# Keeping attention's mixed values on chip and moving their division into the probability flips

## The chip, the cores and the metric

The kernel runs on one core of one Trainium2 chip. The metric is device microseconds of one whole execution, and smaller is better. Its engines are named as in the profile: PE is the matmul engine (PEld its weight loads), DVE the vector engine, ACT the scalar engine, POOL the GpSimd engine, SP the engine whose queue issues most transfers.

## The reference, cut to what matters

One encoder layer with the same weights is applied to a prompt group (512 tokens) and a sample group (1024 tokens), both of width 1024.

```python
oa = _window_attention(qa, ka, va, sink_a)          # 8 heads of 64, 128-token windows, softmax with a sink
ob = _neighbourhood_attention(qb, kb, vb, rpb_b)    # 8 heads of 64, 2-D neighbourhoods, softmax with a bias
merged = concatenate([_rmsnorm(oa, g_out_a), _rmsnorm(ob, g_out_b)], axis=-1)
x = x + merged @ w_out
h = _rmsnorm(x, g_ffn)
x = x + expert_choice_ffn(h, w_router, w_gate, w_up, w_down)   # 16 experts, top-k by token
y = _rmsnorm(x, g_final)
```

## The kernel before

The program runs four stages one after the other, each closed by a barrier of all engines: `project` (the first linear layer), `attend` (both attentions), `mix` (norms, the w_out projection, the router), `experts` (the expert layers and the final norm). Matmuls that must be close to fp32 are made of three passes with operands split in a high and a low part (`three_pass`): high by high, high by low, low by high. A split is one ACT copy (the high part) and one DVE subtraction (the low part).

In `attend` the work is a list of 24 blocks (12 windows and 12 neighbourhoods, taken in turns), each with four head pairs: 96 units. Each engine walks the same list of steps, each lagging by some steps. In its step u, PE makes the two score matmuls of unit u (L922, into one of three score banks), turns the probabilities of unit u-2 (L932, "flips", 12 or 8 transposes into two flip banks), turns the mixed values of unit u-4 (L943), and multiplies values by flipped probabilities for unit u-3 (L963, into one bank). DVE adds mask or bias and takes the row maximum (L863, twice), inverts the sums (L870), copies half of the flips out of PSUM (L875) and scales the output by the inverted sums (L890). ACT copies the other half of the flips (L814), copies the mixed values out so that PE can turn them (L820), and takes the exponentials with their sums (L828). The scaled rows go to DRAM (`o_scratch`), 24 stores. PE fills its gaps at the end of the stage with idle matmuls (L905). In these last steps tile 0 of the stored rows is loaded and turned, and the first two of eight pieces of w_out are split.

In `mix` the rows of 12 token tiles come back from `o_scratch`. Step s works on three tiles: it projects tile s (48 matmuls of 512 columns: eight pieces j of w_out by two column halves by three passes), routes tile t = s-1, and prepares tile s+1. For the preparation ACT squares the row halves, takes the roots, multiplies the rows by the inverse roots (L1190, `ld_merged`), PE turns them (`turn_merged`, L164), ACT makes the high part (L1165) and DVE the low part (L1236, `lower`). For the routing DVE adds the projection to x (L1269), PE turns the sum (L164 with `k_p`), ACT copies it (L1144), PE multiplies by the router (L1404, L1411), DVE reduces (L1312), ACT takes exponentials, DVE scales, and PE turns the result (L1419) in front of the last piece of the step's projection. DVE and ACT take their instructions strictly in the order written. From step 9 on DVE also searches for the best tokens of the sample group between these operations. Tiles 0 and 1 are the exception: their two column groups of `merged` are projected into separate banks, and DVE multiplies by the inverse roots while adding (L1251, L1259).

## Time and profile before

| what | value |
|---|---|
| runs of the kernel | 2483.61, 2486.14, 2487.29 us (median 2486.14) |
| the profiled execution | 2484.71 us, its span 2482.9 us |
| PE busy over the span | 2434.5 us, 98% |
| DVE, ACT, POOL busy | 67%, 59%, 7% |
| `attend`, first score matmul to the last | 315.6 to 494.0 us |
| `mix`, first matmul to the start of `experts` | 502.4 to 682.6 us |

The span is from the first to the last instruction; the 1.8 us between span and time lie around it. Starts of instructions are counted from the span's start. A PE that is busy is not at its peak, since matmuls overlap; so the spacing of starts is what is read below.

### The profile page before, as it was taken

The numbers are of one execution on the slowest core, as the hardware profiler recorded it, in microseconds if no ns is written. First come the engines' busy times: TensorE is split into PE (matmuls) and PEld (weight loads), VectorE is DVE, ScalarE is ACT, GpSimd is POOL, SyncE is SP. The second block draws the span as 40 slices with busy tenths as digits, with TensorE's granted clock in tenths as the row PEclk, the third lists the DMA queues.
The fourth block names the chain that finished last, engine by engine and source line by source line (L and its number), as shares of the span: only waits on it lengthen the run. The fifth ranks groups of instructions, "written<-read, shape, count | busy, mean of one in ns | idle before, by whom it ended". The sixth has DMA issues, their size and how long they took to land.

```text
span 2482.9 us, 43086 instructions
## 1 busy us (share of the span) xinstructions
PE 2434.5 (98%) x16395; PEld 2178.7 (88%) x16395; DVE 1673.5 (67%) x2432; ACT 1456.5 (59%) x2050; POOL 163.7 (7%) x172
## 2 busy tenths in 40 slices
PE   9999999999889999999999999999999999999997
PEld 7888877777579989899998989999998989999896
DVE  6355278854776767676666767666676767666677
ACT  4332189977555656556565656555565655656574
POOL 0000000000010101101010100101010110101010
PEclk9999999999989999999999999999999999999998
DMA  7353255354376767767676767767676776767696
GB/s 250 123 177 113 62 163 202 122 186 154 111 286 224 260 224 258 240 241 247 234 248 233 250 234 248 256 230 251 223 259 226 256 244 238 251 230 253 228 325 222
DMA packets 104549, 545.29 MB, mean 220 GB/s; under 512 B 11344, under 2 KB 19920, under 8 KB 54800
## 3 DMA queue, kind: packets, MB, share of 16 engines
q1 hardware_dynamic: 97072, 518.19, 59.6%
q0 software_dynamic: 7392, 25.96, 4.5%
q8 instruction: 54, 0.88, 0.1%
q14 instruction: 31, 0.25, 0.0%
HBM read 503.21 MB, written 40.89 MB: 219 GB/s over the span
## 4 chain that ended last, share of the span: by engine, by line
PE 69%; DVE 1%; DMA 1%; ACT 1%; issue 0%; POOL 0%; SPq 0%; DVEq 0%; ACTq 0%
PE ex_gate_ps L2043 16%; PE ex_up_ps L2043 16%; PE ex_gate_ps L2045 7%; PE ex_up_ps L2045 7%; PE ex_down_ps L2058 2%; PE ex_down_ps L2062 2%; PE ex_down_ps L2059 2%; PE ex_down_ps L2060 2%; PE ex_down_ps L2063 2%; PE ex_up_ps L2058 2%; PE ex_up_ps L2062 2%; PE ex_up_ps L2063 2%; PE ex_up_ps L2060 2%; PE ex_up_ps L2059 2%; DMA fi_x<-acc_scratch 1%; PE ex_turn_ps L2011 0%
## 5 line engine op out<-in xcount | busy, mean ns | idle before, releaser
L1879 DVE TENSOR_TENSOR ex_w_lo<-ex_w,ex_w_hi 128x2048 fp32r<-128x2048 f32 x384 | 879.8, 2292 | 440.5 <-ACT ex_w_hi L1775 437.1
L1775 ACT ACTIVATE ex_w_hi<-ex_w 128x2048 fp32r<-128x2048 f32 x384 | 733.4, 1910 | 208.7 <-PE ex_down_ps L2063 106.8
L2043 PE MATMUL ex_gate_ps<-ex_xt,ex_w_hi 128*128 128x384 f32 x2048 | 591.8, 359 | 0.7 <-DVE ex_xt L1885 0.7
L2043 PE MATMUL ex_up_ps<-ex_xt,ex_w_hi 128*128 128x384 f32 x2048 | 592.1, 359 | 0.0
L2045 PE MATMUL ex_up_ps<-ex_xt,ex_w_lo 128*128 128x192 f32 x2048 | 512.7, 250 | 0.0
L2045 PE MATMUL ex_gate_ps<-ex_xt,ex_w_lo 128*128 128x192 f32 x2048 | 512.7, 250 | 0.0
L2045 PEld LDWEIGHTS ex_gate_ps<-ex_xt,ex_w_lo 128*128 128x128 f32 x2048 | 391.1, 191 | 0.6
L2045 PEld LDWEIGHTS ex_up_ps<-ex_xt,ex_w_lo 128*128 128x128 f32 x2048 | 391.2, 191 | 0.0
L2043 PEld LDWEIGHTS ex_gate_ps<-ex_xt,ex_w_hi 128*128 128x128 f32 x2048 | 384.5, 188 | 1.6 <-issue 1.0
L2043 PEld LDWEIGHTS ex_up_ps<-ex_xt,ex_w_hi 128*128 128x128 f32 x2048 | 384.5, 188 | 0.0
L1797 ACT ACTIVATE ex_up_low<-ex_up_ps 128x384 f32<-128x384 f32 x128 | 62.9, 492 | 207.8 <-PE ex_up_ps L2045 207.8
L1795 ACT ACTIVATE ex_gate_low<-ex_gate_ps 128x384 f32<-128x384 f32 x128 | 63.0, 492 | 206.0 <-PE ex_gate_ps L2045 206.0
L469 DVE TENSOR_TENSOR pj_w_lo<-pj_w,pj_w_hi 128x1024 fp32r<-128x1024 f32 x54 | 66.2, 1225 | 146.9 <-ACT pj_w_hi L393 146.5
L393 ACT ACTIVATE pj_w_hi<-pj_w 128x1024 fp32r<-128x1024 f32 x54 | 57.1, 1057 | 128.4 <-PE pj_out L198 92.2
L1700 POOL DMA_INDIRECT acc_scratch<-ex_y_s,ex_scatter_s x15 | 24.3, 1619 | 1421.4 <-DVE ex_y_p L1939 1421.4
L1906 DVE TENSOR_TENSOR ex_up_sum<-ex_up_ps,ex_up_low 128x384 f32<-128x384 f32 x128 | 71.4, 558 | 50.7 <-ACT ex_up_low L1797 50.7
L828 ACT ACTIVATE at_probs<-at_raw,at_neg_top 128x385 f32<-128x385 f32 (+5 forms) x192 | 105.4, 553 | 0.2
L2058 PE MATMUL ex_down_ps<-ex_w_hi,ex_ht 128*128 128x512 f32 x256 | 101.7, 397 | 0.0
L2062 PE MATMUL ex_down_ps<-ex_w_hi,ex_ht 128*128 128x512 f32 x256 | 100.0, 391 | 0.0
L2059 PE MATMUL ex_down_ps<-ex_w_lo,ex_ht 128*128 128x512 f32 x256 | 100.0, 390 | 0.0
L2060 PE MATMUL ex_down_ps<-ex_w_hi,ex_ht 128*128 128x512 f32 x256 | 99.8, 390 | 0.0
L2063 PE MATMUL ex_down_ps<-ex_w_lo,ex_ht 128*128 128x512 f32 x256 | 99.6, 389 | 0.0
(310 smaller groups left out, 4012.3 us busy)
## 6 DMA issues: line engine op xcount, KB each, us to landing
ex_w<-in_w_experts SPq DMA_DIRECT2D x384, 1024.0 KB, 4.8
pj_w<-in_w_in SPq DMA_DIRECT2D x54, 512.0 KB, 3.7
pj_xr<-in_xt SPq DMA_DIRECT2D x12, 512.0 KB, 6.0
o_scratch<-ld_out SPq DMA_DIRECT2D x24, 256.0 KB, 4.6
at_bias<-in_near_bias SPq DMA_DIRECT2D x4, 1536.0 KB, 8.8
q_p<-in_x SPq DMA_DIRECT2D x12, 512.0 KB, 4.5
acc_scratch<-k_p SPq DMA_DIRECT2D x12, 512.0 KB, 5.4
h_scratch<-q_p SPq DMA_DIRECT2D x12, 512.0 KB, 3.0
```

The lines of the kernel that those rows point to most:

```text
L469: dve.tensor_tensor(w_lo[:, i % W_SLOTS, :, :].rearrange("p j c -> p (j c)"), w[:, i % W_SLOTS, :], w_hi[:, i % W_SLOTS, :, :].rearrange(" ...
L828: act.activation(probs[:, (2 * u + h) % PROBS, 0:n], raw[:, 2 * pair + h, NEAR_KEYS - b.keys:NEAR_KEYS - b.keys + n], ACT.Exp, bias=neg_to ...
L1775: act.activation(w_hi[:, c % SLOTS, :], w[:, c % SLOTS, :], ACT.Copy).then_inc(hi_w, 1)
L1879: dve.tensor_tensor(w_lo[:, c % SLOTS, :], w[:, c % SLOTS, :], w_hi[:, c % SLOTS, :].bitcast(F32), ALU.subtract).then_inc(lo_w, 1)
L1906: dve.tensor_tensor(up_sum[:], up_ps[:, :, 0:CAP], up_low[:], ALU.add).then_inc(up_summed, 1)
L2043: nc.tensor.matmul(out[:, b, 0:2 * CAP], w_hi[:, slot, f], xt[:, k, :, :].rearrange("p h c -> p (h c)"), start=k == 0, stop=False)
L2045: last = nc.tensor.matmul(out[:, b, 0:CAP], w_lo[:, slot, f], xt[:, k, 0, :], start=False, stop=k == DT - 1)
L2058: nc.tensor.matmul(out[0], s_hi, hi, start=start, stop=False)
L2059: nc.tensor.matmul(out[0], s_hi, lo, start=False, stop=False)
L2060: done = nc.tensor.matmul(out[0], s_lo, hi, start=False, stop=stop)
L2062: nc.tensor.matmul(out[1], both, hi, start=start, stop=False)
L2063: done = nc.tensor.matmul(out[1], both, lo, start=False, stop=stop)
```

## The change

`attend` no longer stores rows. The inverted sums of a unit (two numbers per query) are spread over 128 columns by POOL into `wide`, and PE turns `wide` along with the probabilities of that unit into the same flip banks, as one more block of 64 columns in each. The copies out of PSUM carry that block too. DVE then multiplies the mixed bank by the turned inverses and writes the product over the unit's own queries, which nobody reads any more (`kept`). The transposes of the mixed values, their ACT copies and the stores fall away. The mixed bank and the score banks become two and four; the flip slots three of seven blocks; the bias slots two. The value matmuls come one step later (unit u-4).

In `mix` the values lie turned already, so nothing is loaded and nothing is turned there. Every tile is projected in two parts (A: pieces 0 to 3, B: pieces 4 to 7), and DVE multiplies each part by its inverse root while adding it to x, four operations per tile. The squares are taken on ACT from the turned values, folded on POOL (two additions per tile), and summed across partitions by PE with a column of ones (`tally`, four small matmuls per pair of tiles). Part A of tile 0 and the first five splits of w_out move into the last steps of `attend`; the fills there go from four calls to one.

```diff
+class Mixed:
+    PARTS = 1 + 2
...
 def attend(nc, d, keep, shared, lead):
...
-        PROBS, STATS, BIASES, V_SLOTS, SCORES = 4, 8, 3, 2 * len(V_TILES), 3
+        PROBS, STATS, BIASES, V_SLOTS, SCORES, WIDES = 4, 8, 2, 2 * len(V_TILES), 4, 4
-        FLIP, WEIGH, OUT, STEPS = 2, 4, 4, N + 4
+        INVERT, FLIP, WEIGH, OUT = 1, 2, 3, 4
+        STEPS = N + OUT + 1
...
         @block.scalar
...
-                v = u - WEIGH + 1
-                if 0 <= v < N:
-                    act.wait_ge(weighed, v + 1)
-                    if v >= 2:
-                        act.wait_ge(o_turned, v - 1)
-                    act.activation(o_turn[:, v % 2, :], mixed_ps[:, 0:P], ACT.Copy).then_inc(o_copied, 1)
...
                 if u == N - 1:
+                    act.wait_ge(kept, PAIRS * (FIRST_TILES + 1))
+                    for dst, src in mixed.parts(0, lead.m_hi):
+                        act.activation(dst, src, ACT.Copy).then_inc(lead.hi_m, 1)
+                if u == EARLY_SPLIT:
                     split(0)
+                if N <= u < N + LEAD_SPLITS - 1:
+                    split(u - N + 1)
+        @block.gpsimd
+        def _(pool):
+            for v in range(N):
+                pool.wait_ge(inverted, v + 1)
+                if v >= WIDES:
+                    pool.wait_ge(flipped_ps, 2 * (v - WIDES + 1))
+                pool.tensor_copy(wide[:, v % WIDES, :].rearrange("p (h e) -> p h e", h=2),
+                                 rden[:, v % STATS, :].unsqueeze(2).broadcast_to([P, 2, HD])).then_inc(widened, 1)
         @block.vector
...
+                    dve.wait_ge(flipped_ps, 2 * v + 2)
+                    if v >= FLIPS:
+                        dve.wait_ge(kept, v - FLIPS + 1)
+                    dve.tensor_copy(flip_to(v, 1), flip_from(v, 1)).then_inc(copied[1], 1)
+                if 0 <= u - INVERT < N:
+                    v, r = u - INVERT, (u - INVERT) % STATS
                     dve.wait_ge(exped, 2 * v + 2)
                     dve.reciprocal(rden[:, r, :], sums[:, r, :]).then_inc(inverted, 1)
+                if 0 <= u - OUT < N:
+                    v = u - OUT
+                    dve.wait_ge(weighed, v + 1)
+                    dve.tensor_tensor(queries(v, slice(0, P)), mixed_ps[v % 2][:, 0:P],
+                                      flipped[:, v % FLIPS, 2 * units[v][0].tiles, :], ALU.mult).then_inc(kept, 1)
...
         @block.tensor
...
+                    pe.wait_ge(widened, v + 1)
+                    c = slice(2 * tiles * HD, (2 * tiles + 1) * HD)
+                    turned = [nc.tensor.transpose(flip_ps[i][:, c], wide[ROWS[i], v % WIDES, :], ident[ROWS[i], ROWS[i]])
+                              for i in range(2)]
...
-                if u >= N:
-                    fill(3 if u < STEPS - 1 else 8)
+                    pe.wait_ge(lead.lo_m, Mixed.PARTS)
+                    fill(3)
+                j = u - N - 1
+                if 0 <= j < QA:
+                    pe.wait_ge(lead.lo_w, j + 1)
+                    for k in range(2):
+                        c = slice(k * D // 2, (k + 1) * D // 2)
+                        last = three_pass(nc, score[k][:], (lead.m_hi[:, j, :], lead.m_lo[:, j, :]),
+                                          (lead.w_hi[j][:, c], lead.w_lo[j][:, c]), j == 0, j == QA - 1)
...
 def mix(nc, d, keep, route, shared, lead):
...
+            for t in range(TILES):
+                own = squares[:, t % 2, :, :].rearrange("p (l j) c -> p l j c", l=2)
+                pool.wait_ge(mixed_squared, Mixed.PARTS * (t + 1))
+                pool.tensor_tensor(own[:, :, 0:2, :], own[:, :, 0:2, :], own[:, :, 2:4, :], ALU.add).then_inc(paired, 1)
+                pool.wait_ge(paired, t + 1)
...
+                pool.tensor_tensor(partial[:, t % (2 * PAIR), :, :], own[:, :, 0, :], own[:, :, 1, :],
+                                   ALU.add).then_inc(folded, 1)
...
+            for j in range(LEAD_SPLITS, DT):
                 split(j)
+                if j < DT - 1:
+                    square_mixed(j - LEAD_SPLITS)
             raise_m(1)
...
-                    if t < LAST:
-                        scale_h(t)
-                        search(s, 1)
-                        if n < TILES:
-                            lower(n)
-                    if t == 0:
-                        add_a(1)
+                if t < LAST:
+                    scale_h(t)
+                    search(s, 1)
+                    if n < TILES:
+                        lower(n)
+                    add(s, A)
+                dve.wait_ge(routed, t + 1)
+                dve.tensor_reduce(neg_raw[:], bank[6][:, LOGITS], AX.X, ALU.max,
+                                  negate=True).then_inc(topped, 1)
...
-                    if n < TILES:
-                        turn_merged(n)
```

## Rows read from the trace of the kernel before

**Rows 1.** Windows: stretch, length, busy us of PE, PEld, DVE, ACT, POOL, clock, DMA.

```profile
315.60:494.00 178.40, 177.91 (x2556) 131.23 (x2556) 155.74 (x659) 161.26 (x561) 0.00 (x0) 1.00 0.50 161
...
502.40:531.70 29.30, 27.64 (x164) 20.91 (x165) 21.06 (x42) 20.54 (x39) 1.18 (x3) 0.94 0.56 193
531.70:655.00 123.30, 123.28 (x894) 94.37 (x893) 68.23 (x217) 90.56 (x189) 0.00 (x0) 1.00 0.47 150
```

**Rows 2.** Timeline of PE, step 1 of mix.

```profile
522.55 0.71 PE L164 MATMUL mx_ps<-ident,ld_merged 64*128 64x64 f32 x16 [1.61 <-ACT ld_merged L1190]
```

**Rows 3.** Timeline, two steps of attention: start, us, engine, line, operation.

```profile
399.97 0.92 PE L922 MATMUL at_score<-k_s,q_s 64*128 64x384 f32 x4
...
401.03 0.56 DVE L863 CUSTOM_DVE_ANT_0 at_raw<-at_score,at_bias 128x384 f32<-128x384 f32 x1 [0.30 <-PE at_score L922]
...
401.09 0.23 PE L943 MATMUL at_out<-ident,at_o_turn 64*128 64x64 f32 x2
...
402.06 0.54 DVE L875 COPY at_flipped<-at_flip 128x384 f32<-128x384 f32 x1
...
402.52 0.28 DVE L890 TENSOR_TENSOR ld_out<-at_out,at_rden 128x128 f32<-128x128 f32 x1
...
403.17 0.23 PE L943 MATMUL at_out<-ident,at_o_turn 64*128 64x64 f32 x2
```

**Rows 4.** Timeline, one steady step of mix.

```profile
578.29 0.71 PE L164 MATMUL mx_ps<-ident,k_p 64*128 64x64 f32 x16
578.84 0.66 PE L164 MATMUL mx_ps<-ident,ld_merged 64*128 64x64 f32 x16
...
579.77 0.39 PE L197 MATMUL mx_ps<-ld_w_lo,mx_m_hi 128*128 128x512 f32 x1
580.00 0.40 PE L198 MATMUL mx_ps<-ld_w_hi,mx_m_lo 128*128 128x512 f32 x1
...
580.01 1.09 ACT L1165 ACTIVATE ld_m_hi<-mx_ps 128x512 fp32r<-128x512 f32 x2
580.65 1.29 DVE L1236 TENSOR_TENSOR ld_m_lo<-mx_ps,ld_m_hi 128x512 fp32r<-128x512 f32 x2 [1.45 <-ACT ld_m_hi L1165]
...
583.77 0.29 PE L1411 MATMUL mx_ps<-mx_gather_parts,mx_parts 128*128 128x16 f32 x2
...
584.10 0.17 DVE L1312 TENSOR_REDUCE mx_neg_raw<-mx_ps 128x1 f32<-128x16 f32 x1 [2.17 <-PE mx_ps L1411]
...
585.54 0.28 PE L1419 MATMUL mx_ps<-ident,mx_aff 128*16 128x128 f32 x1
```

**Rows 5.** Timeline, DVE's inversion in two successive steps of a short window.

```profile
423.17 0.16 DVE L870 RECIPROCAL at_rden<-at_sums 128x2 f32<-128x2 f32 x1
...
424.69 0.16 DVE L870 RECIPROCAL at_rden<-at_sums 128x2 f32<-128x2 f32 x1
```

**Rows 6.** Groups of POOL over the whole span: busy us, mean ns, idle before.

```profile
L1695 POOL COPY ex_gate_s<-gates 128x1 f32 x15 | 2.6, 173 | 0.0
...
L1728 POOL TENSOR_TENSOR fi_x<-ex_y_s,fi_gain 128x512 f32<-128x512 f32 x1 | 1.3, 1294 | 0.0
```

**Rows 7.** Timeline, end of attention to the second tile's projection.

```profile
493.97 0.59 PE L922 MATMUL at_score<-k_p,q_p 64*128 64x192 f32 x4
...
496.54 1.14 ACT L805 ACTIVATE ld_w_hi<-q_s,gain_out 128x1024 fp32r<-128x1024 f32 x1
...
502.25 6.07 DVE L1229 SCALAR_TENSOR_TENSOR ld_w_lo<-q_s,gain_out,ld_w_hi 128x1024 fp32r<-128x1024 f32 x5 [0.35 <-PEq L698]
...
514.46 0.19 PEld L196 LDWEIGHTS mx_ps<-ld_w_hi,mx_m_hi 128*128 128x128 f32 x1
```

**Rows 8.** Timeline, DVE beside two POOL additions near the end of the span.

```profile
2458.85 2.10 DVE L212 TENSOR_SCALAR fi_tmp<-fi_ss 128x3 f32<-128x3 f32 x1
```

**Rows 9.** Groups of mix: DVE's addition of a scaled half.

```profile
L1251 DVE SCALAR_TENSOR_TENSOR k_p<-mx_ps,ld_rs,q_p 128x512 f32<-128x512 f32 x4 | 2.8, 746 | 0.0
```

**Rows 10.** Waits in attention, first to last score: total us, times, longest.

```profile
PEld at_score L922 <- DVE at_neg_top L863: 6.0, 32, 0.7
```

More of the change, by code:

```diff
@@ new lines, with __init__, parts @@
+class Mixed:
+    PARTS = 1 + 2
+    def __init__(self, q):
+        self.q = q
+    def parts(self, t, dst):
+        rows, tile = slice(0, P), self.q.at(slice(0, P), slice(0, QA), t * P, P)
+        pieces = [(dst[:, 0:QA, :], tile)]
+        g, first = divmod(t, G_TILES)
+        strips = self.q.at(rows, slice(QA, DT), g * GROUP, GROUP).rearrange(
+            "p j (s r c) -> p j s r c", s=STRIPS, r=Q_ROWS)
+        into = dst[:, QA:DT, :].rearrange("p j (r s c) -> p j r s c", r=2, s=STRIPS)
+        return pieces + [(into[:, :, r, :, :], strips[:, :, :, 2 * first + r, :]) for r in range(2)]
@@ L1330, in _ @@
         def _(pe):
-            def project(s, k, tiles):
-                c = slice(k * HALF, (k + 1) * HALF)
-                for j in tiles:
-                    if s < FIRST:
-                        out, start, stop = (A_BANKS if j < 4 else B_BANKS)[s], j % 4 == 0, j % 4 == 3
-                    else:
-                        out, start, stop = bank_of(s), j == 0, j == DT - 1
-                    last = three_pass(nc, bank[out + k][:], (m_hi[s % 2][:, j, :], m_lo[s % 2][:, j, :]),
-                                      (w_hi[j][:, c], w_lo[j][:, c]), start, stop)
-                return last
@@ L1344, in open_tile @@
-            def open_tile(tiles):
-                halves = [slice(k * HALF, (k + 1) * HALF) for k in range(2)]
-                for j in tiles:
-                    out, start, stop = (A_BANKS if j < 4 else B_BANKS)[0], j % 4 == 0, j % 4 == 3
-                    pe.wait_ge(hi_w, j + 1)
-                    for k in range(2):
-                        nc.tensor.matmul(bank[out + k][:], m_hi[0][:, j, :], w_hi[j][:, halves[k]], start=start, stop=False)
-                    for k in range(2):
-                        nc.tensor.matmul(bank[out + k][:], m_lo[0][:, j, :], w_hi[j][:, halves[k]], start=False, stop=False)
-                    pe.wait_ge(lo_w, j + 1)
-                    for k in range(2):
-                        last = nc.tensor.matmul(bank[out + k][:], m_hi[0][:, j, :], w_lo[j][:, halves[k]], start=False, stop=stop)
-                return last
@@ new lines, in open_pair, with tally @@
+            def open_pair(s, part):
+                if 2 * s + part >= 3:
+                    before, its_part = divmod(2 * s + part - 3, 2)
+                    pe.wait_ge(summed, summed_with(before, its_part))
+            def tally(i):
+                pe.wait_ge(folded, PAIR * (i + 1))
+                for t in range(PAIR * i, PAIR * (i + 1)):
+                    for part in (A, B):
+                        col = 2 * (t % PAIR) + part
+                        last = nc.tensor.matmul(ss1[:, col:col + 1], partial[:, t % (2 * PAIR), part, :], ones[:],
+                                                start=True, stop=True)
+                last.then_inc(tallied, 1)
@@ L1407, in _ @@
                     last.then_inc(parted, 1)
-                both(s, range(3, 5))
+                if s < TILES:
+                    project(s, B, pieces[3:5])
                 if 0 <= t:
@@ L1412, in _ @@
                                      stop=True).then_inc(routed, 1)
[L1413 to L1416 removed]
+                    if s % 2 and s + 2 < TILES:
+                        tally((s + 1) // 2)
+                if s < TILES:
+                    project(s, B, pieces[5:7])
                 if 0 <= t:
@@ L1420, in _ @@
                                         ident[:]).then_inc(aff_turned, 1)
-                last = both(s, range(7, 8))
-                if 0 <= s < TILES:
-                    last.then_inc(projected, 1)
+                if s < TILES:
+                    project(s, B, pieces[7:8])
+                if s == 0:
+                    pe.wait_ge(ready, 1)
+                    tally(0)
 class Choice:
```

565 lines of the change are left out of this document (238 added, 327 removed).

## The prediction

> **What bounds the kernel now.** I read the page first (PE is busy 98% of the span), then the windows by stage, since the change touches only the time from 315.6 to 682.6 us. In attention PE is busy 177.91 of 178.40 us, and in the steady part of mix 123.28 of 123.30 us [rows 1]. So in both stages only what shortens the sequence on PE shortens the kernel, or what lengthens a wait lengthens it. The one stretch with slack is between them, 502.4 to 531.7: PE is busy 27.64 of 29.30 us and the granted clock is 0.94 on the mean. 6% of 29.3 us is 1.8 us lost to the lower of the two clock levels (1.2 GHz in place of 2.4), and it follows a wait of 1.61 us for `ld_merged` [rows 2]. Next I read the timeline of one step of attention and one of mix, to see what stands in front of what. A long step of attention lasts 2.08 us (401.09 to 403.17, the same transposes one step later [rows 3]). A steady step of mix starts with the turn of the sums at 578.29 and passes the turned router result at 585.54 [rows 4].
>
> **Attention, PE.** The change takes away two 64x128 transposes per unit (L943) and adds two of the same shape for `wide`, in the same place of the step, behind the flips. The other matmuls stay. With 0.5 us of idle PE in the stage, the gain is at most 0.5 us. The ACT copies and the stores that go were off this path: they are worth nothing here, and PE's full row is the work that hides them.
>
> **Attention, the new chain.** `wide` brings a chain that was not there: scores of unit u, then DVE's two maxima, its flip copy, its inversion of unit u-1, POOL's spread, and PE's turn in the next step. PE is queued behind that wait with the value matmuls and all later scores. I work it out for a long step. The scores start at 399.97 and DVE's maxima at 401.03; the flip copy now comes before the inversion, so it starts near 402.0. It took 0.46 us to the next start for 384 columns (402.06 to 402.52), so 0.54 us for 448 [rows 3]. The inversion takes 0.16 us [rows 5] and is done near 402.7, 2.7 us after the scores. POOL's copy of 128x128 isn't in the trace. From below it is 0.17 us, a copy of one column; from above 0.46 us, that plus a quarter of what 512 columns of an addition cost over it ((1.29 - 0.17) x 128/512 = 0.28, rounded up) [rows 6]. A copy reads one operand where the addition reads two, so I take 0.3 us. With 0.1 us for two signals, `wide` is there 3.1 us after the scores, and PE wants it at 3.2 us (403.17 minus 399.97 [rows 3]). It fits by 0.1 us. Where it is late, the chain spans two steps, so half the lateness is paid per unit: at 0.46 us for POOL, 0.06 us late, 0.03 x 96 = 3 us. In the short units DVE itself is the bound: its step is 1.52 us (423.17 to 424.69 [rows 5]), and 64 more columns cost 0.08 us. A third of the 96 units are short: at most 32 x 0.08 = 2.6 us, less where a neighbourhood's shorter maxima leave room and where the fourth score bank takes waits away. I take +1.0 us for the stage, with -0.5 and +7 as ends.
>
> **The drain and tile 0.** Before, 20.5 us pass from the last scores (493.97) to the second tile's projection (514.46) [rows 7]. I lay the new order on the same clock. The last exponentials end near 496.4 (the split behind them starts at 496.54). Then ACT makes m_hi in three copies, about 1.2 us (two of 512 columns took 1.09 us; one of 512 and two of 256 have one more start [rows 4]), and DVE m_lo in three, about 1.25 us (two took 1.29 us): 498.9. PE waits for that at step N, so the last flips come near 499.5 and some 2 us of PE are empty. ACT's splits 2 to 4 (1.14 us each) and DVE's low parts (6.07/5 = 1.21 us each [rows 7]) follow the last flip copies. PE's four pieces of part A, 6 matmuls of 0.23 us each (579.77 to 580.00 [rows 4]), 1.4 us a piece, alternate with the last value matmuls and end near 507.3. Then the barrier (0.4 us). In mix ACT has three splits with two sets of squares between them (three activations, 1.2 us a set) and m_hi of tile 1. They end near 508.8, 511.1, 513.5 and 514.7, DVE's low parts 1.3 us later each, and PE's pieces follow those. The tally costs about 0.5 us (eight passes of 0.07 us, half of the 0.14 us between L1411 at 583.77 and the next matmul). So tile 1's projection starts near 516.8, 2.3 us later. In return its step, 17.25 us before (514.46 to 531.7), loses the wait of 1.61 us, the turn of `merged` and the low clock: 5.5 us of part A, 7.3 us from the turn of the sums to L1419, 0.8 us to the end and 0.3 us of waiting for the roots make 13.9 us. Step 2 starts near 530.7, 1.0 us earlier. But the empty 2 us and the three gaps of about 1 us are as long as the wait that went before the low clock in the old kernel [rows 2]. I count one such stretch: +1.8 us; the ends are 0 and two of them, 3.6 us.
>
> **POOL beside DVE.** A DVE operation on three columns took 2.10 us while POOL made two additions [rows 8], where one on two columns takes 0.16 us [rows 5]. In tile 0's step the folds of tiles 0 and 1 (1.29 us for 512 columns, and half of that for 256) meet DVE's low parts of w_out and of tile 1, on which PE waits. Between 0 and one such stall, 2 us, I take +1.0 us. The Trainium skill, page "SBUF — State Buffer", section "Who interferes with whom", says that GpSimd and a DVE instruction with two SBUF inputs, or in a two-port mode, lock each other out for a whole instruction. Rows 8 agree in kind; no row shows a subtraction blocked, and by the rule alone this term would be about 1.3 us, one POOL addition.
>
> **A steady step of mix.** What goes is the turn of `merged`, 0.55 us of PE (that of the sums before it takes 578.29 to 578.84 and has as many instructions [rows 4]). What comes is DVE's `add(s, A)`, twice 0.75 us [rows 9], between `lower` and the router's reduction. Before, `lower` ran from 580.65 to 581.94, and the reduction waited for PE until 584.10: 2.17 us were free. Now m_hi comes from three copies right behind ACT's copy of the sums, so at about 581.3; `lower` takes about 1.25 us to 582.6, the two additions 1.4 us to 584.0. The reduction stands at 584.0 where it stood at 584.10. From it to L1419 are 1.44 us (584.10 to 585.54), and PE, which would be there 0.55 us earlier, waits. So the step keeps its length: I take -0.07 us x 10 = -0.7 us. The tallies (0.5 us in every second step) hide in that same wait; if the wait goes, they count. The ends: -0.55 x 10 + 0.5 x 4 = -3.5 us if DVE's part is hidden, +4 us if each of its operations is 0.1 us slower (four per step).
>
> **The sum.** +1.0 (attention) - 1.0 (drain and step 1) + 1.8 (clock) + 1.0 (POOL beside DVE) - 0.7 (mix) = +2.1 us. The profiled execution took 2484.71 us (span 2482.9) and would take 2486.8; the median, 1.4 us above it, 2488.2 us. That is +0.08%: no change that can be told, since this kernel's runs tell differences of about 0.2% (5 us) from none.
>
> **Rivals.** First, faster: PE's loads of score weights wait 6.0 us for DVE's maxima with three banks [rows 10], and the fourth bank and the missing copy on ACT free them. Without my +1.0 that gives 2488.2 - 1.0 - 6.0 = 2481.2 us. For it speaks the number of waits, 32, as many as there are short units. Against it: these are waits of the loads, under running matmuls; PE's own idle is 0.5 us [rows 1]. It decides if the short steps fall by 0.15 us or more. Second, slower: `wide` is late in every step. At 0.2 us late (POOL's copy 0.6 us, or slow signals, which the trace doesn't show for POOL in such a loop) 0.1 x 96 = 9.6 us are paid: 2488.2 - 1.0 + 9.6 = 2496.8 us. The margin of 0.1 us speaks for it, the 0.17 us copies against it. Third, the drain: if mix's first fold isn't ready when tile 0 is, PE and with it everything waits. A POOL that starts its additions 3 us late moves step 1 by about 2.5 us: 2490.7 us. No row shows a first addition that anyone waited for. The Trainium skill, "GPSIMD Engine Reference", section 2.1 ("Instruction dispatch"), states about 6 us for the first call of a freshly loaded kernel; nothing here shows it, and by it the fold would be some 2.6 us late, an estimate from that page. Fourth, the change's aim, a shorter step of mix by the missing turn: 2488.2 - 2.8 = 2485.4 us, within the same bound.
>
> **Chances.** My sum, or the fourth or third rival with nothing else, within 0.2%: 0.50. Faster (the first rival, or mix, clock and stalls all at their good ends, 2488.2 - 2.8 - 1.8 - 1.0 - 1.5 = 2481.1): 0.17. Slower (the second rival, or both stretches of low clock with a late fold and a late DVE in mix, 1.8 + 2.5 + 2 on top of the sum): 0.33. The range reaches down to the faster cases' edge, 2481, and up to the second rival, 2497; the ends beyond have about 2 in 10.
>
> **What would show it.** In attention the step stays 2.08 us and PE's transposes of `wide` follow the flips without a gap; a gap before them that names POOL is the second rival. In mix the reduction follows `add(s, A)` directly, DVE no longer idles before it, and PE's L1419 transposes wait for DVE; if the step is 13.2 us, I mis-sized DVE's part. Between them, the low clock should lie near 500 us and not near 524. I am wrong if POOL's copy is much over 0.3 us, if PE's short steps shrink, or if the splits in the drain cost PE more than the 2 us of empty time.

## The result and the profile after

The changed kernel takes 2492.36 us (median of ten runs, 2489.95 to 2494.95); the kernel before, in ten runs beside it, 2484.07 us. The ratio is 1.0033 with an interval of 1.0024 to 1.0042: 8.3 us slower. The forecast was 2488.2 us, +2.1 us on its own base, in a range of 2481 to 2497.

The profiled execution took 2494.95 us, the longest of the ten, with a span of 2492.8 us, so its stages add up to 9.9 us and not to 8.3. A part of the loss lies in no stage: around the span stand 2.1 to 2.2 us in every run of the changed kernel and 1.7 to 1.9 us in every run of the kernel before, which is 0.4 us of the 8.3. The windows below cut both traces at the same events: the first and the last unit's scores, mix's first projection, the second tile's projection, the turn of the first router result (L1419 before, L1372 after) and that of the last one. Columns as in [rows 1]. The kernel before, with these cuts:

```profile
315.60:493.97 178.37, 177.88 (x2554) 131.20 (x2554) 155.71 (x659) 161.26 (x561) 0.00 (x0) 1.00 0.50 161
493.97:502.39 8.42, 7.60 (x105) 5.35 (x104) 4.77 (x20) 7.12 (x21) 0.19 (x1) 1.00 0.89 285
502.39:514.46 12.07, 12.02 (x64) 9.32 (x65) 10.81 (x10) 10.06 (x17) 1.19 (x3) 1.00 0.80 293
514.46:530.82 16.36, 14.74 (x98) 10.85 (x96) 10.27 (x32) 9.92 (x21) 0.00 (x0) 0.90 0.40 129
530.82:676.79 145.97, 139.60 (x1013) 106.30 (x1012) 86.08 (x270) 103.23 (x213) 0.00 (x0) 0.98 0.43 138
```

The changed kernel:

```profile
315.14:499.03 183.89, 180.85 (x2559) 133.51 (x2559) 162.91 (x660) 152.80 (x473) 27.04 (x93) 0.99 0.41 134
499.03:515.17 16.14, 13.63 (x95) 9.63 (x94) 9.86 (x24) 7.97 (x19) 0.91 (x5) 0.79 0.11 34
515.17:525.20 10.03, 7.27 (x32) 5.15 (x33) 6.61 (x6) 7.90 (x13) 7.11 (x8) 1.00 0.50 173
525.20:538.53 13.33, 13.33 (x89) 10.37 (x89) 10.74 (x28) 8.41 (x20) 4.10 (x4) 1.00 0.36 130
538.53:685.48 146.95, 138.35 (x902) 105.61 (x900) 97.06 (x275) 89.53 (x188) 16.31 (x16) 0.99 0.29 107
```

Attention is 5.5 us longer (183.89 to 178.37), the stretch from the last scores to the first router result 2.65 us (39.50 to 36.85), the rest of mix 1.0 us (146.95 to 145.97). Attention starts 0.5 us earlier, and behind mix 1.2 us are lost; 5.5 + 2.65 + 1.0 - 0.5 + 1.2 = 9.9 us. The last two are scatter: over all profiled executions of this and the following kernels attention starts at 314.5 to 316.0 us (315.60 before), and 1805.8 to 1807.5 us follow mix (1806.1 before). What is to be explained is 9.2 us in three stretches.

**Attention.** (The section on the change has the value matmuls come one step later. By the code they stay where they were: `u - WEIGH + 1` with `WEIGH` 4 and `u - WEIGH` with 3 are both unit u-3. Nothing below hangs on it.) The spread is what the prediction took it for. Its row in POOL's groups over the whole span:

```profile
L845 POOL COPY at_wide<-at_rden 128x128 f32<-128x128 f32 x96 | 27.9, 291 | 473.5 <-DVE at_rden L882 473.5
```

PE's waits from the first to the last scores (total us, times, longest):

```profile
PE at_flip L930 <- issue: 2.2, 1, 2.2
...
PE at_flip L936 <- POOL at_wide L845: 0.2, 1, 0.2
```

POOL's copy takes 0.29 us, and PE waits for it once, 0.2 us. The wait to look at is the other: once 2.2 us ahead of the flips, with no releaser named. The timeline at that place, in step 80 and the two steps behind it:

```profile
471.21 1.14 ACT L808 ACTIVATE ld_w_hi<-ld_w,gain_out 128x1024 fp32r<-128x1024 f32 x1
...
472.03 0.70 PE L920 MATMUL ld_open<-k_p,q_p 64*128 64x256 f32 x4
472.25 0.42 ACT L817 ACTIVATE at_flipped<-at_flip 128x320 f32<-128x320 f32 x1
472.39 1.28 DVE L895 SCALAR_TENSOR_TENSOR ld_w_lo<-ld_w,gain_out,ld_w_hi 128x1024 fp32r<-128x1024 f32 x1 [1.37 <-ACT ld_w_hi L808]
473.59 0.48 DVE L869 CUSTOM_DVE_ANT_0 at_raw<-at_score,band,at_neg_sink 128x256 f32<-128x256 f32 x1
...
474.40 0.48 DVE L878 COPY at_flipped<-at_flip 128x320 f32<-128x320 f32 x1
...
474.99 0.46 PE L930 MATMUL at_flip<-ident,at_probs 64*128 64x64 f32 x8 [2.25 <-issue]
```

This is the first split of w_out, which the change moved from the end of the stage into step 80. DVE takes its list in order, so it stands 1.37 us until ACT's high part is there, though the scores of unit 81 lie ready behind it; it works 1.28 us on the low part, and only then takes the maxima of unit 81 and copies the flips of unit 79 out of PSUM (474.40 to 474.88). PE, in step 82, has made the scores of unit 82 and needs that bank for the flips of unit 80: they start at 474.99. Their exponentials had been done since 471.2, and those of unit 81 end at 475.17, so it was the bank that PE waited for. Then the granted clock falls (windows of 2 us, columns as above):

```profile
474.00:476.00 2.00, 1.01 (x18) 0.91 (x18) 2.00 (x12) 1.42 (x5) 0.29 (x1) 1.00 1.07 389
476.00:478.00 2.00, 2.00 (x26) 1.52 (x22) 1.56 (x8) 1.50 (x7) 0.29 (x1) 0.64 0.49 190
478.00:480.00 2.00, 2.00 (x18) 1.28 (x16) 0.61 (x3) 1.00 (x5) 0.29 (x1) 0.51 0.01 4
```

A clock of 0.51 is the lower level, 1.2 GHz. The time from the scores of unit 80 to those of unit 88 grew by 4.4 us, from 13.26 to 17.63 us; 0.6 us of that is there without the split, too (13.85 us in E1 below), and the rest is the gap and the slow stretch.

**The drain.** PE stands empty again, this time ahead of the last unit's flips, until the low part of tile 0 is there; part A of tile 0 then starts at half speed.

```profile
502.42 1.36 DVE L891 TENSOR_TENSOR ld_m_lo<-q_s,ld_m_hi 128x512 fp32r<-128x512 f32 x3
...
503.92 0.80 PE L905 MATMUL at_score<-ident 128*128 128x256 bf16 x3 [1.87 <-DVE ld_m_lo L891]
...
506.40 0.80 PE L196 MATMUL ld_open<-ld_w_hi,ld_m_hi 128*128 128x512 f32 x1
506.99 0.63 PE L197 MATMUL ld_open<-ld_w_lo,ld_m_hi 128*128 128x512 f32 x1
...
511.06 0.39 PE L198 MATMUL ld_open<-ld_w_late,ld_m_lo 128*128 128x512 f32 x1
```

The 0.63 us of a matmul of 512 columns at 507 and the 0.39 us at 511 are the two levels; the windows show 0.50 from 503.90 to 510.30.

**Mix.** Two steps of the steady part, PE:

```profile
593.40 0.27 PE L1372 MATMUL mx_ps<-ident,mx_aff 128*16 128x128 f32 x1
...
606.79 0.28 PE L1372 MATMUL mx_ps<-ident,mx_aff 128*16 128x128 f32 x1 [0.25 <-DVE mx_aff L1292]
...
618.33 0.29 PE L1364 MATMUL mx_ps<-mx_gather_parts,mx_parts 128*128 128x16 f32 x2
618.47 1.03 PE L1326 MATMUL mx_ps<-mx_ones,mx_partial 128*128 128x1 f32 x8
619.36 0.48 PE L196 MATMUL ld_open<-mx_w_hi,mx_m_hi 128*128 128x512 f32 x1
...
620.83 0.27 PE L1372 MATMUL mx_ps<-ident,mx_aff 128*16 128x128 f32 x1
```

Without tally a step takes 13.39 us (593.40 to 606.79) and PE waits 0.25 us for DVE at its end. With tally it takes 14.04 us and PE doesn't wait; the tally holds PE for 0.89 us (618.47 to 619.36). Two old steps were 27.36 us, two new ones are 27.43 us. The old ones are counted from this line to the one at 585.54 in [rows 4], four steps:

```profile
530.82 0.28 PE L1419 MATMUL mx_ps<-ident,mx_aff 128*16 128x128 f32 x1
```

### The profile page after: what moved, and what is told of

It is laid out like the page before. It is cut to its first block, busy times and chain, and to the rows that moved or that the text cites. A ratio compares the mean times of both kernels' runs of the same rounds, so it can differ in the third digit from the quotient of the medians.

```text
span 2492.8 us, 42529 instructions
## 1 busy us (share of the span) xinstructions
PE 2436.7 (98%) x16237; PEld 2180.2 (87%) x16237; DVE 1693.0 (68%) x2434; ACT 1431.4 (57%) x1929; POOL 219.6 (9%) x293
## 4 chain that ended last, share of the span: by engine, by line
PE 69%; DVE 1%; DMA 1%; ACT 1%; issue 0%; SPq 0%; POOL 0%; DVEq 0%; ACTq 0%
PE ex_gate_ps L1998 16%; PE ex_up_ps L1998 16%; PE ex_gate_ps L2000 7%; PE ex_up_ps L2000 7%; PE ex_down_ps L2013 2%; PE ex_down_ps L2017 2%; PE ex_down_ps L2014 2%; PE ex_down_ps L2015 2%; PE ex_down_ps L2018 2%; PE ex_up_ps L2018 2%; PE ex_up_ps L2014 2%; PE ex_up_ps L2015 2%; PE ex_up_ps L2017 2%; PE ex_up_ps L2013 2%; DMA fi_x<-acc_scratch 1%; PE ex_turn_ps L1966 0%
```

## The experiments

All times are beside runs of the kernel before on the same chip. "Attention" is from the first to the last unit's scores, "drain" from there to mix's first projection, "tile 0" from there to the end of the first tally, "mix" from the first to the last turn of a router result, each in the profiled execution. The intervals of most of these rows overlap; the lengths of a stage with the same code, where the clock doesn't come in, agree between executions within 0.5 us, and the verdicts rest on them. The numbers are those of the runs as they were named; there is no E3.

| kernel | median us | ratio (interval) | attention | drain | tile 0 | mix |
|---|---|---|---|---|---|---|
| the changed kernel | 2492.36 | 1.0033 (1.0024 to 1.0042) | 183.89 | 16.14 | 10.03 | 146.95 |
| E1 split in the drain | 2489.19 | 1.0022 (1.0013 to 1.0031) | 180.14 | 14.68 | 10.00 | 146.98 |
| E2 wait at part A | 2490.24 | 1.0026 (1.0016 to 1.0036) | 184.00 | 11.98 | 10.00 | 146.97 |
| E4 additions late | 2492.89 | 1.0038 (1.0025 to 1.0052) | 184.12 | 13.20 | 9.98 | 147.13 |
| E5 low part later | 2491.92 | 1.0033 (1.0021 to 1.0045) | 181.13 | 14.76 | 10.03 | 146.96 |
| E6 = E1 + E2 | 2488.09 | 1.0019 (1.0010 to 1.0028) | 180.33 | 14.55 | 10.01 | 146.98 |
| E7 = E6, additions late but the last | 2488.66 | 1.0021 (1.0012 to 1.0030) | 180.56 | 13.02 | 10.00 | 146.92 |
| E8 one tally of four | 2492.07 | 1.0037 (1.0023 to 1.0051) | 183.97 | 15.94 | 10.00 | 145.45 |
| E9 no first folds | 2492.72 | 1.0039 (1.0025 to 1.0052) | 183.95 | 14.67 | 9.15 | 146.96 |
| E10 = E6, idle matmuls | 2487.73 | 1.0016 (1.0007 to 1.0025) | 180.26 | 12.98 | 10.00 | 146.96 |
| E11 idle matmuls in the gap | 2490.36 | 1.0029 (1.0018 to 1.0040) | 184.04 | 12.68 | 9.99 | 146.94 |
| E12 = E6, narrow copy | 2486.91 | 1.0015 (1.0006 to 1.0024) | 178.80 | 13.06 | 9.99 | 146.96 |
| E13 = E10, squares later | 2487.36 | 1.0016 (1.0007 to 1.0025) | 180.39 | 12.99 | 9.70 | 146.95 |

My theory after the result: most of the 8.3 us is the split in step 80 with the low clock behind it, the next part PE's wait in the drain with a second stretch of low clock, and about 1 us the tally. The rivals were the short windows themselves, POOL's spread or POOL beside DVE, and DVE's additions in mix.

**E1: the split back in the drain.** In ACT's list, and the same two lines in DVE's:

```diff
-                if u == EARLY_SPLIT:
-                    split(0)
-                if N <= u < N + LEAD_SPLITS - 1:
-                    split(u - N + 1)
+                if N <= u < N + LEAD_SPLITS:
+                    split(u - N)
```

> The changed kernel with the first split of w_out taken out of step 80 of attention: ACT and DVE make splits 0 to 4 in steps 96 to 100, one each. Theory: in the changed kernel ACT's high part (1.14 us) and DVE's low part (1.28 us) of that split stop the two engines in the middle of short steps; PE stands still for 2.25 us at 472.73, then runs at half clock from 476 to 480, and the units from 472 to 486 take 4.4 us longer than before. Without it these units take what they took before (last scores near 494.9 instead of 499.3), and the drain gets at most 1.2 us longer: 3.2 us less in all (2.0 to 4.4), a ratio to the kernel before near 1.0020. Rival: the stall comes from the loads of w_out that arrive from 469 to 477, or from the short windows themselves; then it stands at the same place, and the ratio stays near 1.0033.

The stage lost 3.75 us, the median 3.2 us (by the ratios to the kernel before, 1.0022 against 1.0033, it is 2.7 us). PE's gap and the low clock near 472 are gone:

```profile
315.36:495.50 180.14, 179.34 (x2558) 132.67 (x2558) 161.83 (x659) 151.78 (x472) 27.07 (x93) 1.00 0.42 136
```

The clock of the stage is 1.00 again. The rival is out: the loads and the short windows are still there. The remaining 1.8 us over [rows 1]'s stage are E12's subject.

**E5: only DVE's half of the split moved.** ACT's high part stays in step 80, DVE's low part goes three steps on, so that it doesn't stand in front of ready work until ACT is done.

```diff
-                if u == EARLY_SPLIT or N <= u < N + LEAD_SPLITS - 1:
+                if u == EARLY_SPLIT + 3 or N <= u < N + LEAD_SPLITS - 1:
```

> The changed kernel with DVE's low part of split 0 three steps behind ACT's high part (step 83 instead of 80); ACT's high part stays in step 80. Theory: half of PE's gap at 472.73 is DVE standing 1.37 us for ACT's high part, on which nothing else in the step depends; with the low part later DVE loses only its own 1.28 us, PE's gap falls from 2.25 us to about 0.9 us, and with a short gap the half clock does not come: 1.4 to 3.1 us less, a ratio of 1.0021 to 1.0027. Rival: it is ACT's 1.14 us ahead of its flip copy that stops PE; then the gap stays above 1.5 us, the half clock too, and the ratio is 1.0033.

In the stage the theory holds: 181.13 us, 2.8 less than in the changed kernel, and PE is full where it stood still:

```profile
472.00:474.00 2.00, 2.00 (x30) 1.36 (x28) 1.91 (x11) 2.00 (x7) 0.29 (x1) 1.00 1.06 358
474.00:476.00 2.00, 2.00 (x30) 1.53 (x26) 1.82 (x10) 2.00 (x9) 0.29 (x1) 1.00 1.10 383
```

So ACT's 1.14 us alone stops nobody; it was DVE's wait for it, plus DVE's own 1.28 us. The latter still costs: behind the low part, now in step 83, PE stands 0.73 us (0.9 was expected), and the clock stays up. The median shows only 0.4 us of this in six runs, and the ratio none (1.0033); the interval just contains the 2.8 us. I keep the stage's reading, which is that of one execution, and leave the median's open.

**E2, E11: the wait in the drain and the clock behind it.** E2 moves the wait, E11 leaves it where it is and fills the empty stretch.

```diff
                     pe.wait_ge(added, 2 * N)
-                    pe.wait_ge(lead.lo_m, Mixed.PARTS)
                     fill(3)
                 j = u - N - 1
+                if j == 0:
+                    pe.wait_ge(lead.lo_m, Mixed.PARTS)
```

And E11:

```diff
+                    fill(16)
                     pe.wait_ge(lead.lo_m, Mixed.PARTS)
-                    fill(3)
```

> The changed kernel with PE's wait for the low part of tile 0 moved from before the last unit's flips to just ahead of the first piece of part A; the three idle matmuls stay in front of the flips. Theory: PE stands empty from 502.05 to 503.92 for that wait, and the half clock from 504 to 510.3 follows from it. Moved, the flips start near 502.9, part A near 504.4 instead of 506.40, at full clock, and the barrier of attention passes near 511.3 instead of 514.9: 3.5 us less (2.5 to 4.5), a ratio near 1.0019. Rival: DVE's chain of low parts sets the pace of part A anyway, the wait comes back at the first piece and the clock falls all the same: 0 to 1 us less, a ratio of 1.0029 to 1.0033.

> The changed kernel with sixteen idle matmuls ahead of PE's wait for tile 0's low part, in place of three behind it. Nothing waits less: the wait stands where it stood. Theory: the half clock of the drain (504 to 510 us in the changed kernel's profile) follows the empty stretch of 1.85 us; with the stretch filled it does not come, and the time from the last scores to mix's first projection is 13.2 us, as in the one profiled execution with the same drain in which the clock stayed up, and not 14.6 to 16.1 as in the others: 1.7 us less on the median (0.8 to 3), a ratio near 1.0026. Rival: the clock falls for another reason (the half clock in attention before it, or the rows of short matmuls), and filling changes nothing: 1.0033.

The drains of the two, from the last scores to mix's first projection, E2 first:

```profile
499.35:511.33 11.98, 10.85 (x96) 7.78 (x94) 9.60 (x24) 7.87 (x19) 0.91 (x5) 1.00 0.14 45
```

```profile
499.81:512.49 12.68, 12.05 (x109) 9.04 (x107) 9.69 (x24) 7.97 (x19) 0.91 (x5) 1.00 0.14 43
```

Both ran at full clock; E2 took 4.2 us off the profiled drain of the changed kernel, E11 3.5 us, and the medians fell by 2.1 and 2.0 us (by the ratios 1.7 and 1.0 us, with intervals that overlap that of the changed kernel). That idle work alone shortens the drain by 3.5 us suggests that most of the loss was the clock, but one execution of E11 doesn't show it: five profiled executions have the drain of the changed kernel unchanged, gap and all, and they took 16.14, 14.76, 15.94, 14.67 and, in E4, 13.20 us. E4's was at full clock from end to end:

```profile
498.79:511.99 13.20, 10.70 (x96) 7.79 (x94) 9.69 (x24) 7.98 (x19) 0.91 (x5) 1.00 0.14 41
```

E1's drain has the same empty stretch of 1.87 us, and the low clock behind it (14.68 us). The low clock behind this gap thus came in five of six executions, and costs 0 to 2.9 us. It doesn't hang on the low clock in attention, E11's rival: E1 and E5 had none there and fell in the drain, E4 had it and did not. The moved wait by itself is worth 1.2 us (13.20 to 11.98).

**E6, E10: both edits, and idle matmuls ahead of part A.** E10 adds `fill(12)` behind the moved wait.

> The two edits of before together: all five splits of w_out in steps 96 to 100, and PE's wait for tile 0's low part just ahead of part A. Theory: they cost in two different places and add up. The first alone took the last scores 3.8 us nearer to the first (180.14 us, 183.89 in the changed kernel) and the median 2.7 us down by its ratio; the second took the low clock out of the drain and 1.7 us off the median. Together 4.4 us (3 to 6): a ratio near 1.0016. Rival: with the split in the drain DVE's low parts set the pace of part A whether or not PE waits earlier, so that the second edit gives nothing more: a ratio of 1.0022, and a gap ahead of part A that names the low part of w_out.

> The kernel with the wait moved and the split in the drain, with twelve idle matmuls (0.11 us each) on PE between the wait for tile 0's low part and the wait for the first low part of w_out. Theory: its profiled execution ran at half clock from 501.9 to 505.3 behind an empty stretch of 1.37 us in that place; with PE busy there the half clock does not come, and the 12 matmuls end when the low part is there. The half clock cost 1.7 us where it came; it did not come in every execution, so 0.8 us less on the median (0.3 to 1.7): a ratio near 1.0016. Rival: the idle matmuls only push part A back by what they take over the gap, and the clock falls behind another gap: 1.0019 or more.

E6's 1.0019 lies midway between the sum (1.0016) and the split alone (1.0022), and the interval doesn't part them. Its profiled execution has the rival's gap and the low clock behind it: the drain took 14.55 us, with PE waiting for the first low part of w_out:

```profile
501.34 0.47 PE L196 MATMUL ld_open<-ld_w_hi,ld_m_hi 128*128 128x512 f32 x1 [1.37 <-DVE ld_w_lo L893]
```

With that gap filled (E10) the drain took 12.98 us at full clock and the ratio was the expected 1.0016. But E7 and E12 have E6's drain with the gap unfilled, and they took 13.02 and 13.06 us, at full clock too. So what the fill does is not shown here: where the clock stays up it gives nothing, and whether it kept the clock up in E10 one can't tell from an execution in which it might have stayed up anyway.

**E9: POOL's first folds.** A constant is written instead of the two additions for tiles 0 and 1.

```diff
                 pool.wait_ge(mixed_squared, Mixed.PARTS * (t + 1))
+                if t < 2:
+                    pool.memset(partial[:, t, :, :], 4.0).then_inc(folded, 1)
+                    continue
```

> The changed kernel without POOL's folds of tiles 0 and 1 (a constant is written in their place, so the roots of these two tiles are not the right ones). Theory: while these folds run, DVE's low parts in front of part B of tile 0 take 1.38 and 2.13 us instead of 1.28, and that of tile 1 takes 1.89 us instead of 1.36; PE waits for the second (1.27 us at 522.88). Without the folds DVE's operations take 1.28 and 1.36 us, PE's gap falls to about 0.4 us, and step 1 starts 0.9 us earlier: a ratio near 1.0029. Rival: PE waits in that place for ACT's high parts, which stand behind the squares, and DVE's longer operations are hidden by them: the same start of step 1, a ratio of 1.0033.

POOL and DVE in the changed kernel, as tile 0's part B is prepared (POOL's own fold of 256 columns takes 0.74 us elsewhere):

```profile
518.51 1.38 DVE L1217 SCALAR_TENSOR_TENSOR ld_w_late<-v_s,gain_out,mx_w_hi 128x1024 fp32r<-128x1024 f32 x1 [0.89 <-ACT mx_w_hi L1141]
...
518.88 1.60 POOL L1121 TENSOR_TENSOR mx_partial<-mx_squares 128x256 f32<-128x256 f32 x1
...
520.69 2.13 DVE L1217 SCALAR_TENSOR_TENSOR ld_w_late<-k_s,gain_out,mx_w_hi 128x1024 fp32r<-128x1024 f32 x1 [0.80 <-ACT mx_w_hi L1141]
...
521.82 1.59 POOL L1121 TENSOR_TENSOR mx_partial<-mx_squares 128x256 f32<-128x256 f32 x1
...
522.75 1.89 DVE L1224 TENSOR_TENSOR mx_m_lo<-q_s,mx_m_hi 128x512 fp32r<-128x512 f32 x3
```

And E9:

```profile
519.28 1.28 DVE L1220 SCALAR_TENSOR_TENSOR ld_w_late<-k_s,gain_out,mx_w_hi 128x1024 fp32r<-128x1024 f32 x1 [0.89 <-ACT mx_w_hi L1144]
520.49 1.36 DVE L1227 TENSOR_TENSOR mx_m_lo<-q_s,mx_m_hi 128x512 fp32r<-128x512 f32 x3
```

Alone, DVE takes 1.28 and 1.36 us; beside the folds 2.13 and 1.89. PE's three gaps in part B, 0.87, 0.61 and 1.27 us, became 0.88, 0.50 and 0.50 us, and tile 0 got 0.9 us shorter (9.15 us where the changed kernel takes 10.03), as expected; the rival is out. Five runs of the whole can't show 0.9 us, and their median doesn't.

**E13: the same cost by order.** In E10's kernel ACT's squares of tile 1 go behind the last split.

```diff
             for j in range(LEAD_SPLITS, DT):
                 split(j)
-                if j < DT - 1:
-                    square_mixed(j - LEAD_SPLITS)
+                if j == LEAD_SPLITS:
+                    square_mixed(0)
+            square_mixed(1)
```

> The kernel with the idle matmuls ahead of part A, and in mix ACT's squares of tile 1 behind the last split of w_out instead of between the last two. Theory: PE's gaps in tile 0's part B (0.87, 0.61 and 1.27 us in the changed kernel's profile) are DVE's low parts, which stand behind ACT's high parts, which stand behind the squares; POOL's folds then lengthen the last by 0.85 us. With the squares later the last low part is ready 1.2 to 2 us earlier, the tally waits for the folds instead, and step 1 starts 1.0 us earlier (0.3 to 1.3): a ratio 0.0004 below that of the kernel with the idle matmuls alone, near 1.0012. Rival: the folds come so late that the tally and the low parts of tile 1 wait as long as PE did: the same.

Tile 0 got 0.3 us shorter (9.70 us, 10.00 in E10), the low end of what was expected: the second gap became 0.63 us, the third vanished, but the tally now waits 0.71 us for POOL, and DVE's low part of tile 1 takes 2.65 us beside the later folds. The rival had the larger part of it.

**E4, E7: DVE's additions.** E4 puts the two additions of part A behind the router's scaling in every step; E7 does so in E6's kernel and leaves the last step as it was.

```diff
                     if n < TILES:
                         lower(n)
-                    add(s, A)
...
                 dve.tensor_scalar(aff[:, t % 2, :], e_aff[:], e_inv[:], None, ALU.mult).then_inc(aff_made, 1)
+                if t < LAST:
+                    add(s, A)
```

> The changed kernel with DVE's two additions of part A in mix (1.40 us a tile) moved from between the low parts and the router's reduction to behind the router's scaling. Theory: in every second step of mix (those without tally, 13.39 us) PE waits 0.26 us for DVE ahead of L1372, because the additions hold back the reduction; without them in that place the step takes 13.13 us and the others stay at 14.05: 5 x 0.26 = 1.3 us less, a ratio near 1.0028. Rival: the additions free a bank or lead to the next part B, so that a later wait takes the place of the one removed: 0 us, or up to 3 us more.

> The same with DVE's additions of part A behind the router's scaling in every step of mix but the last, where they stay ahead of the reduction. Theory: the steps without tally fall from 13.39 to 13.13 us as they did with the additions late, and the last step keeps its 9.85 us (it rose to 11.21 with them late): 1.25 us less than with the first two edits, a ratio near 1.0011 (1.0000 to 1.0020). Rival: the gain of 0.25 us a step is taken back where the last additions stand, as in the run with all of them late: no less than the first two edits.

The steps without tally fell to 13.14 us, as the theory said, and PE no longer waits there (E4):

```profile
589.66 0.27 PE L1373 MATMUL mx_ps<-ident,mx_aff 128*16 128x128 f32 x1
...
602.80 0.28 PE L1373 MATMUL mx_ps<-ident,mx_aff 128*16 128x128 f32 x1
```

The stage as a whole is no shorter (147.13 and 146.92 us). In E4 the last step took 11.21 us instead of 9.85. With the last step kept in E7, the one before it took 14.49 us instead of 13.30, with PE waiting for DVE:

```profile
669.54 0.28 PE L1374 MATMUL mx_ps<-ident,mx_aff 128*16 128x128 f32 x1 [1.17 <-DVE mx_aff L1292]
```

From step 9 on DVE searches for the best tokens and has little free time (in the changed kernel PE already waits 0.92 us for it at the end of step 9); what is put off in steps 1 to 8 costs nothing, what is put off there is paid. The rival was right on the sum and wrong on the place.

**E8: the tally.** One matmul in place of four for pairs 1 to 5.

```diff
+                if i:
+                    last = nc.tensor.matmul(ss1, partial[:, PAIR * i % (2 * PAIR), A, :], ones[:], start=True, stop=True)
-                for t in range(PAIR * i, PAIR * (i + 1)):
+                for t in range(PAIR * i, PAIR * (i + 1) if i == 0 else 0):
```

> The changed kernel with one tally matmul per pair of tiles instead of four for pairs 1 to 5 (its sum serves for all four columns, so the roots are not the right ones). Theory: the four tallies take 0.89 us of PE (eight passes of 0.11 us), of which only the 0.26 us for which PE would wait for DVE are hidden, and that is why every second step of mix takes 14.04 us and not 13.39. With a quarter of them the steps are all near 13.39 us: 5 x 0.65 = 3.2 us less, a ratio near 1.0020. Rival: what makes the longer step is the root behind the tally (ACT's table load, DVE's inversion of four columns), which holds up the chain on DVE; then the steps stay near 14.0 us and the ratio at 1.0033.

```profile
578.45 0.28 PE L1374 MATMUL mx_ps<-ident,mx_aff 128*16 128x128 f32 x1 [0.26 <-DVE mx_aff L1292]
...
592.00 0.28 PE L1374 MATMUL mx_ps<-ident,mx_aff 128*16 128x128 f32 x1
...
605.35 0.28 PE L1374 MATMUL mx_ps<-ident,mx_aff 128*16 128x128 f32 x1 [0.26 <-DVE mx_aff L1292]
```

A step with tally fell from 14.04 to 13.55 us (578.45 to 592.00), the others stayed at 13.4 and still wait for DVE. The theory holds, the rival is out. The stage lost 1.5 us and not 3.2: 0.15 us a step were missing, step 9, the first with the search, rose from 14.06 to 14.56 us, and one of the five tallies lies ahead of the first turn, where the stage begins. The median doesn't show it.

**E12: the longer copies of the short steps.** E6's kernel, with DVE's copy cut by the 64 columns of the turned sums.

```diff
-                    dve.tensor_copy(flip_to(v, 1), flip_from(v, 1)).then_inc(copied[1], 1)
+                    n = 2 * units[v][0].tiles + (v < 8)
+                    dve.tensor_copy(flipped[:, v % FLIPS, 0:n, HD:P],
+                                    flip_ps[1][:, 0:n * HD].rearrange("p (b q) -> p b q", q=HD)).then_inc(copied[1], 1)
```

> The kernel with the wait moved and the split in the drain, but from unit 8 on DVE's copy of the flips leaves out the block of turned sums (64 of 320 or 448 columns), so the queries of one half are scaled by old numbers. Theory: what attention still takes more than before (180.33 us from first to last scores, 178.37 before) is DVE's longer copy in the short steps, 1.65 us where it was 1.52; without the block the short steps are back, 1.2 us less in the stage, a ratio near 1.0014. Rival: ACT's copy of the other half is as much longer, or PE's wait for the spread sums, and sets the same pace: the stage stays at 180.3 us, 1.0019.

```profile
315.03:493.83 178.80, 178.07 (x2559) 133.66 (x2559) 156.42 (x660) 151.75 (x472) 26.86 (x93) 1.00 0.42 137
```

The stage fell by 1.5 us, to within 0.4 us of the old 178.37; that 0.4 us lies in the first six units, where the copy is still whole. So what attention costs beside the split is mostly DVE's 64 columns, and not ACT, POOL's copy or PE's wait for it. By units, the gain is 0.04 to 0.08 us in each of twenty steps, short ones (every second of these came from 1.65 to 1.59 us, not to 1.52) and those where the length of a unit changes; one more step took 2.26 us in E6 and 2.06 us in E1, so against E1 the gain is 1.3 us.

No version beat the kernel before. The best that still does the whole work, E10 and E13, are 0.16% behind it: 1.9 us of attention, 1.0 us of mix, and in the profiled execution of E10 0.6 us less from the last scores to the first router result. That is 2.3 us of the 4.1 us between the medians; the profiled execution of before was 1.1 us over its median and that of E10 the lowest of its eleven, so the rest, but for the 0.4 us around the span, can't be placed.

## Why the prediction was right and where it was wrong

The time fell in the range, and the sign of the sum was right, but the likeliest case was no change that can be told and the result is one of +0.33%. That the range held it is luck: its upper end stood at 2497 for the second rival, a `wide` that is late in every step, which did not occur; the largest part of the loss is a cost that is in no term. By its steps:

- **Attention, +1.0 forecast, +5.5 measured. This is the step that failed, by one part of the change that it never priced.** It lists what PE, DVE and POOL get for `wide`, and then costs "ACT's splits 2 to 4" in the drain. The split of step 80 stood in the diff, but not in the sum: 1.14 us of ACT and 1.28 us of DVE among short steps, in which the text itself called DVE the bound. E1 prices it at 3.75 us of the stage, PE's wait for the flip bank and the low clock behind it; E5 shows that DVE's stand for ACT, with that clock, is the larger part of it. The rest, 1.3 to 1.5 us by E12, is the "at most 2.6 us" of short steps, mis-sized at 1.0: the 0.08 us a step was about right, and twenty steps pay it and not 32.
- **The new chain: right.** POOL's copy at 0.29 us (0.3 was taken), the two signals around it 0.06 us each (0.1 was taken for both), one wait of 0.2 us, long steps still 2.08 us. The second rival had the right size of loss for a reason that didn't occur.
- **The first rival: out.** With four banks the weight loads of scores still wait for DVE, 3.6 + 2.7 = 6.3 us in 34 waits, where they waited 6.0 us in 32 [rows 10]. So the fourth bank did not free them, and the short steps, which were to fall by 0.15 us, rose from 1.53 to 1.65 us in every second one.
- **The drain and tile 0: right where the clock stayed up.** From the last scores to the second tile's projection 516.8 - 493.97 = 22.8 us were forecast, and 1.0 us more for POOL; E4, the changed kernel's drain at full clock, took 13.20 + 9.98 = 23.2 us, the profiled changed kernel 26.2 us. Up to the first router result E4 took 36.5 us, 0.4 us less than before (36.85), where -1.0 and POOL's +1.0 were forecast.
- **The clock, +1.8 with ends 0 and 3.6: right in kind and place.** In the drain the measured cost lies between 0 (E4) and 2.9 us; the second stretch, behind the split of step 80, belongs to the step that was missed.
- **POOL beside DVE, +1.0: right**, 0.9 us by E9, with a subtraction and a split held up. The Trainium skill, page "SBUF — State Buffer", section "Who interferes with whom", says that a DVE instruction with two SBUF inputs contends with a GpSimd instruction that reads SBUF; a block for the whole instruction it spells out for the two-port modes. The trace agrees in kind: a low part took 0.85 us longer and a fold of 256 columns 0.86 us longer; the rows don't show whether one engine was shut out for a whole instruction of the other.
- **The third rival, a late first fold: out.** POOL began the first fold at 517.52, as soon as the squares were there, and took 1.29 us for it.
- **Mix, -0.7 forecast, +1.0 measured: mis-sized.** Three terms were off. The step without tally gained 0.29 us and not 0.07. The tally costs 0.89 us in PE (eight passes of 0.11 us) where 0.5 was taken from passes of 0.07. And it was to "hide in that same wait", which is 0.25 us long. The first eight steps took 4 x (13.39 + 14.04) = 109.7 us, 109.4 before; the other 0.6 us come from the last three, where DVE is full (13.69, 13.19 and 9.73 us before; 14.06, 13.30 and 9.85 us after): PE waits 0.92 us for it at the end of step 9, and not at all there before.

What stays open: why the low clock follows the same gap in some executions only, whether idle matmuls in the gap keep it away, and where E5's gain of 2.8 us in the stage went in its median.

## What to carry to other kernels

When one line of a diff moves a piece of work to an earlier step, price it in the step that it moves into, engine by engine, before anything else: 1.2 us put into the lists of two in-order engines in a stage that is 99% full cost 3.75 us. If the second engine's half needs the first's, place it some steps later, since an in-order engine that waits holds up ready work (E5: 2.8 us of the stage). And where a matmul engine will stand empty for a microsecond or two, count the low clock that may follow, not only the gap: here it added 0 to 2.9 us. Idle matmuls in the gap are a cheap thing to try: the three profiled executions with filled gaps (E10, E11, E13) stayed at full clock in the drain, while of those with the gaps left open three of nine did, so this is a hint and no proof.

## What the runs showed of the hardware

The granted clock after one and the same empty stretch of PE, 1.87 us in the drain, stayed at 1.00 in one profiled execution (E4) and fell to 0.50 in five (the changed kernel, E1, E5, E8, E9), for 3.4 to 6.8 us. After an empty stretch of 2.25 us in attention it fell in all six executions that had one, for 3.4 us; after one of 1.37 us in the drain in one of three (E6, not E7 and E12). A fold of 256 columns on POOL took 0.74 us alone and 1.60 us beside DVE's split, and the split 2.13 us where it takes 1.28 us alone. Eight matmul passes with a single moving column took 0.11 us each, so that four sums of 128 tokens cost 0.89 us.
